# Feed-forward gate and up tiles of a two-block transformer: single runs, or runs of two tiles that take turns

## What is computed

```python
def swiglu(x, w_gate, w_up, w_down):
    return (jax.nn.silu(x @ w_gate) * (x @ w_up)) @ w_down

for l in range(DEPTH):          # first block; the second has the same two around another mixer
    h = h + 0.5 * swiglu(rmsnorm(h, ffn1_norm[l]), ffn1_w_gate[l], ffn1_w_up[l], ffn1_w_down[l])
    h = h + mixer(rmsnorm(h, mix_norm[l]))
    h = h + 0.5 * swiglu(rmsnorm(h, ffn2_norm[l]), ffn2_w_gate[l], ffn2_w_up[l], ffn2_w_down[l])
```

## Time and profile before

| | |
|---|---|
| Time, median of 3 runs | 2158.76 us (2158.53 to 2159.02) |
| The profiled execution's own time | 2158.53 us |
| Its span, first to last instruction | 2156.6 us |
| PE busy | 2151.1 us, 100% of the span, 15592 matmuls |
| PE weight loads (PEld) busy | 2033.0 us, 94% |
| DVE busy | 1560.2 us, 72% |
| ACT busy | 1220.3 us, 57% |
| POOL busy | 470.0 us, 22% |
| DMA | 395.81 MB, mean 184 GB/s |

### The profile page before, as it was taken

One profiled execution on the slowest core, in us unless ns is written; L12 is line 12 of the kernel. 1 busy time (PEld: TensorE's weight loads), 2 busy tenths in 40 slices (PEclk: granted clock), 3 DMA queues, 4 the chain that ended last, 5 costly groups with the idle time before them and its releaser, 6 DMA issues.

```text
span 2156.6 us, 38780 instructions
## 1 busy us (share of the span) xinstructions
PE 2151.1 (100%) x15592; PEld 2033.0 (94%) x15592; DVE 1560.2 (72%) x2591; ACT 1220.3 (57%) x2047; POOL 470.0 (22%) x514
## 2 busy tenths in 40 slices
PE   9999999999999999999999999999999999999999
PEld 9999999999999999988988999889888999999888
DVE  8655977665665587875697587965876688887863
ACT  6544466444544446665566445655655577676652
POOL 1000532520350152231053000430331011101420
PEclk9999999999999999999999999999999999999999
DMA  8645436975785543565465654665555775664753
GB/s 285 217 162 191 140 116 167 231 184 185 193 210 179 169 154 117 185 213 181 164 202 199 200 184 146 224 198 191 181 192 176 210 205 170 180 190 142 229 177 102
DMA packets 424225, 395.81 MB, mean 184 GB/s; under 512 B 16864, under 2 KB 420448, under 8 KB 424048
## 3 DMA queue, kind: packets, MB, share of 16 engines
q1 hardware_dynamic: 410336, 375.22, 55.1%
q0 software_dynamic: 13424, 17.78, 4.0%
q10 hardware_dynamic: 288, 0.34, 0.0%
HBM read 389.65 MB, written 7.41 MB: 184 GB/s over the span
## 4 chain that ended last, share of the span: by engine, by line
PE 98%; DVE 1%; ACT 1%; DMA 0%; issue 0%; SPq 0%; DVEq 0%; ACTq 0%
PE ps L1763 30%; PE ps L1756 26%; PE ps L1758 17%; PE ps L1761 17%; PE ps L1779 1%; PE ps L2106 1%; PE ps L2105 1%; PE ps L2104 1%; PE ps L2072 0%; PE ps L2056 0%; PE ps L1882 0%; PE ps L2085 0%; PE ps L1927 0%; DVE t L1234 0%; PE ps L2039 0%; PE ps L2040 0%
## 5 line engine op out<-in xcount | busy, mean ns | idle before, releaser
L1763 PE MATMUL ps<-t 128*128 128x256 f32 (+1 forms) x5456 | 1402.0, 283 | 0.0
L1763 PEld LDWEIGHTS ps<-t 128*128 128x128 f32 x5456 | 995.0, 188 | 33.8
L1234 DVE TENSOR_TENSOR t<-t 128x1024 fp32r<-128x1024 f32 (+1 forms) x722 | 875.9, 1230 | 155.0 <-ACT t L882 154.4
L882 ACT ACTIVATE t<-t 128x1024 fp32r<-128x1024 f32 (+1 forms) x722 | 728.3, 1030 | 222.9 <-PE ps L1763 216.9
L1756 PE MATMUL ps<-t 128*128 128x512 f32 x2420 | 809.4, 391 | 0.1
L1758 PE MATMUL ps<-t 128*128 128x272 f32 (+1 forms) x3036 | 798.0, 288 | 0.4 <-DVE t L1465 0.3
L1761 PE MATMUL ps<-t 128*128 128x272 f32 (+1 forms) x3036 | 786.0, 284 | 0.0
L1758 PEld LDWEIGHTS ps<-t 128*128 128x128 f32 x3036 | 540.0, 188 | 5.9 <-issue 3.3
L1761 PEld LDWEIGHTS ps<-t 128*128 128x128 f32 x3036 | 542.1, 189 | 0.8
L1756 PEld LDWEIGHTS ps<-t 128*128 128x128 f32 x2420 | 426.2, 188 | 63.2 <-DVE t L1234 0.3
L806 POOL TENSOR_TENSOR t<-t 128x256 f32<-128x256 f32 x110 | 100.3, 912 | 694.7 <-ACT t L1000 694.7
(11 more groups left out here) (208 smaller groups left out, 1583.1 us busy)
## 6 DMA issues: line engine op xcount, KB each, us to landing
t<-ffn_w_in SPq DMA_DIRECT2D x88, 1024.0 KB, 5.3
t<-ffn_w_gate SPq DMA_DIRECT2D x42, 1024.0 KB, 5.2
t<-ffn_w_up SPq DMA_DIRECT2D x42, 1024.0 KB, 7.1
t<-attn_w_qkv SPq DMA_DIRECT2D x72, 512.0 KB, 5.6
t<-ffn_w_down SPq DMA_DIRECT2D x32, 1024.0 KB, 5.3
t<-ffn_w_out SPq DMA_DIRECT2D x32, 1024.0 KB, 5.2
t<-w_in SPq DMA_DIRECT2D x28, 1024.0 KB, 4.9
t<-ffn_w_down SPq DMA_DIRECT2D x16, 768.0 KB, 4.4
```

Source lines behind the costliest of these rows:

```text
L882: act.activation(whi[:, plan.place[n], 0:nk, :], kept(u)[:, 0:nk, half * P:half * P + P], ACT.Copy).then_inc(S["hi"], 1)
L1234: dve.tensor_tensor(wlo[:, plan.place[n], 0:nk, :], kept(u)[:, 0:nk, half * P:half * P + P], f32(whi[:, plan.place[n], 0:nk, :]), ALU.subt ...
L1763: ins = pe.matmul(o, lo, xhi, start=False, stop=i == r.nk - 1)
```

## The change

The table of runs of each feed-forward stage gets, after the first run and single tiles up to the eighth tile, eighteen runs of two in place of thirty-six single tiles. Tiles 8 and 9 (counted from 0), 10 and 11, up to 42 and 43, are now pairs of a gate tile and its up tile.

```diff
                 n = 4 if s else NFIRST
-                for n in [n] + [1] * (2 * FCH - n):
+                for n in [n] + [1] * (8 - n) + [2] * (FCH - 4):
                     self.run(s, n, KC, c0, range(8))
                 for m in range(0, KC, 2):
                     self.run(s, 2, FCH, c0, range(8), m)
```

## The result

| | before | with the change |
|---|---|---|
| Median | 2159.44 us (11 runs) | 2165.64 us (11 runs) |
| Lowest to highest | 2158.53 to 2160.08 us | 2161.44 to 2171.32 us |
| Ratio | | 1.0028 (95%: 1.0021 to 1.0036) |
| Profiled execution, span | 2158.53, 2156.6 us | 2166.04, 2164.1 us |

The kernel is slower, by 6.2 us in the median where 1.3 was forecast, and above the range given. The second thing to see is the spread: 1.6 us between the runs of before, 9.9 us between those of the changed kernel. A mean cost is only half of what has to be explained.

What follows compares the result with a forecast made beforehand. TensorE alone bounds the kernel, so time is the sum of its start-to-start distances. Waits +2.42 and +1.03, faster pairs -1.92, rest 0: +1.5 us on 2158.53, 2160.0 us (+1.3 us on the median); range 2158.4 to 2163.2 us.

Steps and rivals of the forecast that it cites:

- The distance in stages 2 and 3: Pairs in stages 2 and 3 run at 124.45 ns a matmul instead of 125.56: -0.96 us each, -1.92 us.
- The waits: TensorE waits for piece 9 before the first pair at tile 8: +2.42 us in stage 0, +1.03 us in stage 6.
- just even: Stages 5, 8, 11, first pair: piece ready 0.24 us before tile 8 against 0.25 us needed; 0, at most 0.1 each.
- The cover of later pairs: After the first pair, DVE's 12.9 us lead loses up to 6.0 us; seven microseconds are left, so no further waits.
- The clock: Stage 0's wait may bring the granted clock down; as long at half rate as at program start costs up to 2 us.
- rival 2: Pairs of all three wide stages lock at 126.0 ns, +4.7 us with the waits: 2163.2 us; chance 0.08.
- Distance, joined stages: Pairs in the five joined stages keep the single tiles' matmul distance, judged by down tiles: nothing, at most +0.1 us.
- Stage 0: Stage 0's pairs run at 125.5 ns, as good as single tiles: 0, with bounds -0.96 and +0.4 us.
- The range: Whole kernel's time lies between 2158.4 us and 2163.2 us.

Runs made afterwards that it cites:

- the kernel with the added waits: Against the kernel with pairs from tile 16 on in all stages: a short TensorE wait added before the first pair in stages 5, 8, 9 and 11; 2161.84 us.

## Why the prediction was wrong

- **The distance in stages 2 and 3** (-0.96 us each): right, 107.53 for 108.48, and confirmed alone. The reasoning from the down tiles, as pairs that begin straight after single tiles, was the right one.
- **The waits** in stages 0 and 6 (+2.42 and +1.03): right in place and nearly in size, 2.1 and 1.0. Both estimates came of comparing DVE's end of a piece with the start of the tile ahead. In stages 5 and 8 the "just even" was 0.09 us.
- **The cover of later pairs** (seven microseconds left, no further wait): right. PE's weight loads show two long waits for L1234 in all.
- **The clock** was the half of rival 2 that I gave little: "as long again at half rate would cost up to 2 us". In the profiled execution it came, and with the first pair cost 1.6 us; its mark is on 14 of 33 executions with that wait. The trace of before had no wait of that length, so it could only be bounded; it should have been part of the price of the wait, with a chance, and not a step of a rival.
- **The step that failed** is "Distance, joined stages": "nothing, at most +0.1 us". I took the joined down tiles as the nearest row and stopped there, although a few lines on I read from the earlier trace rows that the distance depends on the pattern and that "an interruption can change the pattern". The same text then put an even wait of 0.24 against 0.25 us at the first pair of stages 5, 8 and 11, and priced it by its length, 0.1 each. What that wait can do is tip a whole stage, as it did in stage 11 in the three profiles with joined pairs from tile 8 on: 1.9 us in the pairs and 1.0 to 1.2 in down tiles that the change doesn't touch. Stages 5 and 8 with the same short wait, and stage 6 with 1.0 us, were fast in all three. With one to three stages tipped, as the times with joined pairs alone suggest, this is 3 to 9 us and the largest term of all. The trace of before has no row of the slow joined pattern, so its size was not to be had; that the bound was open upwards was.
- **Stage 0** (taken as 0, between -0.96 and +0.4): the pairs came out at about 0, by luck: 126.1 ns up to tile 15, and 125.6 behind `start_work`, where two other kernels had 126.1. But I left out the down tiles behind them, which inherit the pattern: +0.4 to +0.65 us for three runs, a little more for all four.
- **Rival 2** named the right kind of mechanism, pairs locked in a slow pattern after an interruption, for all three wide stages. It occurred in part of stage 0 and not in stages 2 and 3, and it was not named for the joined stages, where it cost most. Its time of 2163.2 us is nearer to the median than the forecast, but by luck.
- **The range** ended at 2163.2 and assumed a kernel as steady as before. The spread of the changed kernel is itself a result: the number of slow stages changes from one execution to the next. Four first pairs of joined stages are delayed (stage 9's is not); which of them tip in the executions without a trace is not known.

The Trainium skill (TensorE: Matmul & The Clock Gate, Back-to-back issue gap) gives N/2.4 + 2.5 ns as the isolated gap in the warm state, and says that in a stream of weight loads and matmuls both set the spacing. It has one spacing for a width. This trace has three for the same three matmuls of 272 (124.4, 125.6, 126.1) and two for the turn of 512 and 256 (173.4, 176.7), at full granted clock. The measurement decides.

What stays open is where the patterns come from. No run changed an address or a weight load, so I can't say whether reads, weight loads or something else sets them. Nor is it known why a delay tips a run in one execution and not in another.

## What to carry to other kernels

When TensorE is the only bound and has no holes, look at its start-to-start distance in every kind of run, and ask of a new order not only how fast it goes but how it is entered: let it begin behind work that always settles the same way, with all its operands ready, and never with a wait that is "just even". A run that needs two operands at once moves the second one's due time forward by a whole tile, at the place where the producer is furthest behind. And if a change makes the times spread, read the single times before the median: steps of equal size suggest how many places have tipped, and what each costs; a trace has to confirm it.

## What the runs showed of the hardware that was not expected

- The same matmuls in the same order run in one of several steady patterns, chosen when the sequence begins: 124.4, 125.6 or 126.1 ns for 272 columns; 173.4 or 176.7 ns for the mean of 512 and 256. A pattern lasted for 150 us and more, through tile and run boundaries, to the end of the stage or until single tiles came. It even crossed into the next stage: where stage 5's down tiles were slow, in the kernel with the added waits, stage 6's run of four began at 176.6 ns.
- Single tiles by contrast came back to one distance within two tiles, in every feed-forward stage of the profiles read here.
- A delay of about 0.1 us ahead of the first pair was enough to tip it in some stages of a trace and not in others. Delays of 0.5 and 1.0 us, where traces have them (stages 9 and 6), left the pairs fast.
- A wait of 2.1 us (2.22 from start to start) was followed by a granted clock of 0.53 over 3.65 us, 1.2 GHz for most of it, in one trace; two others kept the full clock after 2.25 and 2.54. The mean clock was 0.999 in 14 of 33 executions of these kernels and 1.000 in all 8 whose longest added wait was the 1.0 us of stage 6.
